# The last seven pivots of a small triangular solve move from GpSimd to VectorE

## The reference

```python
kk = jnp.einsum('bhncd,bhnsd->bhncs', k, k)
A = jnp.where(strict, beta[..., :, None] * kk * decay, 0.0)
rhs = jnp.concatenate([v * beta[..., None], k * (beta * jnp.exp(G))[..., None]], axis=-1)
sol = lax.linalg.triangular_solve(eye + A, rhs, left_side=True, lower=True)
```

## Time and profile before

| | |
|---|---|
| median of 3 runs | 2664.82 us (2664.16 to 2670.57) |
| the profiled execution | 2664.91 us, of which the span of its instructions is 2663.4 us |
| PE, PE weight loads | busy 96%, 95% of the span |
| DVE, ACT, POOL | busy 62%, 50%, 20% |
| TensorE clock granted, mean | 0.987 |
| DMA | 189 GB/s of memory traffic over the span |

### The profile page before, as it was taken

How to read it: one execution, slowest core, us unless ns; L and a number is a source line. 1 busy time by engine, 2 the same in 40 slices (tenths; PEclk the granted TensorE clock), 3 DMA queues, 4 the chain that set the end, 5 groups by cost and what they waited for, 6 DMA issues and landing times.

```text
span 2663.4 us, 53087 instructions
## 1 busy us (share of the span) xinstructions
PE 2566.9 (96%) x20849; PEld 2540.5 (95%) x20849; DVE 1661.4 (62%) x2866; ACT 1337.6 (50%) x2030; POOL 529.2 (20%) x910
## 2 busy tenths in 40 slices
PE   6999999999999999999999999999999999999997
PEld 5899999999999999999999999899999999999997
DVE  4858677676867675533355565466676656776665
ACT  5546455464645544443344343355555545665563
POOL 1335271634527160000000000100110000110100
PEclk9999999999999999999999999999999999999999
DMA  5555464655546456667645556656997567986563
GB/s 178 165 144 170 138 189 134 179 149 163 165 140 193 133 167 185 189 197 216 202 154 171 181 166 203 217 167 217 312 311 236 180 198 228 320 284 194 167 194 112
DMA packets 444289, 506.58 MB, mean 190 GB/s; under 512 B 21145, under 2 KB 423714, under 8 KB 441298
## 3 DMA queue, kind: packets, MB, share of 16 engines
q1 hardware_dynamic: 416128, 415.42, 51.9%
q0 software_dynamic: 27408, 88.53, 10.6%
q10 hardware_dynamic: 578, 0.19, 0.0%
HBM read 478.15 MB, written 26.49 MB: 189 GB/s over the span
## 4 chain that ended last, share of the span: by engine, by line
PE 60%; DMA 2%; POOL 1%; issue 1%; DVE 1%; ACT 0%; DVEq 0%; POOLq 0%; ACTq 0%
PE bank L695 60%; DMA raw<-in_w_o 1%; POOL sol L558 1%; POOL prod L555 1%; DMA raw<-in_w_ffn_down 0%; DVE wlo L1302 0%; PE bank L720 0%; ACT whi L982 0%; DMA raw<-in_w_ple_gate 0%; DMA DT<-sol_scratch 0%; DVEq L234 0%; DMA sol_scratch<-sol 0%; DVE xlo L1330 0%; POOL sol_scratch L588 0%; POOL sol L551 0%
## 5 line engine op out<-in xcount | busy, mean ns | idle before, releaser
L695 PE MATMUL bank<-xhi,whi 128*128 128x264 f32 x5520 | 1597.8, 289 | 37.1 <-DVE wlo L1302 16.9
L695 PE MATMUL bank<-xlo,whi 128*128 128x264 f32 x5520 | 1572.7, 285 | 0.0
L695 PE MATMUL bank<-xhi,wlo 128*128 128x264 f32 x5520 | 1570.3, 284 | 0.0
L1302 DVE TENSOR_TENSOR wlo<-raw,whi 128x1024 fp32r<-128x1024 f32 x828 | 1012.8, 1233 | 752.5 <-ACT whi L982 751.6
L982 ACT ACTIVATE whi<-raw 128x1024 fp32r<-128x1024 f32 x828 | 872.7, 1058 | 811.9 <-PE bank L695 728.1
L695 PEld LDWEIGHTS bank<-xhi,whi 128*128 128x128 f32 x5520 | 1046.5, 190 | 41.3 <-issue 40.6
L695 PEld LDWEIGHTS bank<-xlo,whi 128*128 128x128 f32 x5520 | 1046.9, 190 | 2.2 <-issue 1.9
L695 PEld LDWEIGHTS bank<-xhi,wlo 128*128 128x128 f32 x5520 | 1043.4, 189 | 0.0
L695 PE MATMUL bank<-ahi,whi 128*128 128x264 f32 x704 | 200.7, 285 | 2.5 <-DVE wlo L1302 2.5
L695 PE MATMUL bank<-ahi,wlo 128*128 128x264 f32 x704 | 200.8, 285 | 0.0
L695 PE MATMUL bank<-alo,whi 128*128 128x264 f32 x704 | 200.3, 285 | 0.0
(11 more groups left out here) (294 smaller groups left out, 1862.0 us busy)
## 6 DMA issues: line engine op xcount, KB each, us to landing
raw<-in_w_in SPq DMA_DIRECT2D x356, 512.0 KB, 4.0
raw<-in_w_ffn_gate SPq DMA_DIRECT2D x88, 512.0 KB, 5.0
raw<-in_w_ffn_up SPq DMA_DIRECT2D x88, 512.0 KB, 4.6
raw<-in_w_ffn_down SPq DMA_DIRECT2D x96, 384.0 KB, 3.4
raw<-in_w_gdn_out SPq DMA_DIRECT2D x64, 512.0 KB, 3.6
chunkS<-in_state_gdn POOLq DMA_DIRECT2D x16, 1024.0 KB, 7.2
raw<-in_w_sconv_out SPq DMA_DIRECT2D x32, 512.0 KB, 3.6
raw<-in_w_o SPq DMA_DIRECT2D x32, 512.0 KB, 3.8
```

Source lines behind the costliest of these rows:

```text
L695: return pe.matmul(out, lhsT, rhs, start=start, stop=stop)
L1302: dve.tensor_tensor(wlo[:, at_ % SPLIT, :, :], raw[:, at_ % RAW, :, :], f32(whi[:, at_ % SPLIT, :, :]), ALU.subtract).then_inc(lo_ready, 1)
```

## The change

POOL stops after pivot 23 and signals `begun`. A new DVE step `solve`, written into slot 21 behind the split of piece 24, waits for `begun`, does pivots 24 to 30 with the same two operations a pivot, and signals `solved`, for which POOL waits before it stores `sol`. POOL's copy of the unit columns is written ahead of the wait for `blk`.

```diff
+LASTP = 24
...
-        DVE_STEP = {"cur": {0: ("exponents",), 5: ("lt",), 13: ("qn",), 16: ("qkt",), 26: ("mask",), 27: ("e0",),
+        DVE_STEP = {"cur": {0: ("exponents",), 5: ("lt",), 13: ("qn",), 16: ("qkt",), 21: ("solve",), 26: ("mask",), 27: ("e0",),
...
             def solve(grp):
 
+                mine.inc(pool.tensor_copy(sol[:, :, :], unit[:, :, :]))
                 pool.wait_ge(g["blk_in"], grp * 64 + 64)
                 pool.sem_inc(pool_passed, 1)
-                mine.inc(pool.tensor_copy(sol[:, :, :], unit[:, :, :]))
-                for j in range(SB - 1):
+                for j in range(LASTP):
                     n, m = SB - 1 - j, j // 4 + 1
...
                 mine.settle(pool)
-                pool.sem_inc(g["solved"], 1)
+                pool.sem_inc(g["begun"], 1)
...
+                elif slot == "solve":
+                    dve.wait_ge(g["begun"], gr + 1)
+                    for j in range(LASTP, SB - 1):
+                        n, m = SB - 1 - j, j // 4 + 1
+                        mine.inc(dve.tensor_tensor(prod[:, 0:m, 0:n], blk[:, j, j + 1:SB].unsqueeze(1).to_broadcast([P, m, n]),
+                                                   sol[:, 0:m, j:j + 1].to_broadcast([P, m, n]), ALU.mult))
+                        mine.settle(dve)
+                        mm_ = dve.tensor_tensor(sol[:, 0:m, j + 1:SB], sol[:, 0:m, j + 1:SB], prod[:, 0:m, 0:n], ALU.add)
+                        if j < SB - 2:
+                            mine.inc(mm_)
+                            mine.settle(dve)
+                    mm_.then_inc(g["solved"], 1)
```

More of the change, by code:

```diff
@@ L248, in trunk @@
         act_self, dve_self, pool_self = sem("act_self"), sem("dve_self"), sem("pool_self")
-        pool_passed, dve_passed = sem("pool_passed"), sem("dve_passed")
+        pool_passed = sem("pool_passed")
         ident_ready = sem("ident_ready")
@@ L269, in trunk @@
             "rows", "gb", "expo", "dt", "kcopied", "lt", "nturned", "ncopied",
-            "blk_stored", "blk_in", "solved", "sol_stored", "dt_in", "vturned", "vcopied", "pt", "masked",
+            "blk_stored", "blk_in", "begun", "solved", "sol_stored", "dt_in", "vturned", "vcopied", "pt", "masked",
             "t0", "t0c", "pt0", "e0", "pe0", "f0c", "pf0", "u0", "s1", "s1c", "ks", "r",
```

## The result

| | before | after |
|---|---|---|
| median, us | 2664.00 (20 runs, 2657.1 to 2670.57) | 2671.91 (20 runs, 2663.84 to 2681.62) |
| ratio, 95% interval | | **1.0033** (1.0025 to 1.0041) |
| the profiled execution, us | 2664.91 | 2681.62 |
| PE's waits for `DT`, us | 19.5 in 8, longest 6.2 | 25.1 in 8, longest 4.4 |
| falls of the clock behind `pt` | 3 (groups 0, 2, 6) | 6 (groups 0, 2, 3, 4, 5, 6) |

The change makes the kernel 0.33% slower.

The account below looks back on a forecast made before the run. PE, busy 96% of the span, was taken as the bound, with 19.5 us of waits for `DT` to shrink. Gains of 3.6 (group 0), 4.5 (groups 1 to 7) and 3.2 (clock), 11.3 us, gave 2653.6 us, range 2646.5 to 2661.5.

Parts of the forecast that it names:

- the fourteen operations: DVE's pivots 24 to 30, two chained operations each, take 3.1 us in all, between 2.8 and 4.4.
- dear and cheap small operations: Rivals on DVE's operations: dear, up to 0.31 us each, 2675.2 us, chance 0.05; cheap, 0.09 us each, 2641.3 us, chance 0.03.
- what sets the end of the solve: Group 1: DVE's program place, not POOL, sets it; `begun` comes 4.0 us before split 24 ends; store 0.64 us earlier.
- group 0 up to the store: Group 0: DVE waits for POOL, `begun` comes at about 139.95, and the store starts at 143.8, 4.9 us earlier.
- the change doesn't do what it says: Rival: copy hidden in one group of eight, group 0's pivot 23 no sooner; 2655.1 us, inside the forecast, no separate chance.
- PE does not wait for split 25: Split 25, delayed behind DVE's pivots, still has 4 us to spare in group 1 and 2.6 in group 0; costs nothing.
- the step that took the time from store to `DT` as constant: Store to `DT` stays 11.8 us as in group 1; piece 29's load, up to 3.5 us later, costs nothing.
- 4.5 us: Groups 1 to 7: the store of `sol` starts 0.64 us earlier in each, a gain of 4.5 us in all.
- The prediction's own sign of being wrong: Wrong if PE's `DT` waits exceed 15 us, DVE takes over 3.7 us, or PE waits for `wlo` at piece 25.
- two falls of the clock go: Behind `pt` of groups 2 and 6: waits shrink to about 1.4 us, so two clock falls vanish, gaining 3.2 us.
- group 0, wait and clock: Group 0's wait for `DT` shrinks to 2.6 us, gaining 3.6 us, between 2.8 and 4.9; its clock fall is left in.
- given back by the transfers: Rival: in groups 1 to 7 late loads fall on the store and cancel the 0.64 us; 2661.3 us, chance 0.20.

Follow-up runs that it names:

- wait_only: Kernel before, with DVE in groups 1 to 7 waiting for POOL's whole solve ahead of split 25, doing no pivot: 2663.36 us, ratio 0.9995.
- both_no_dve: Kernel before without pivot 30, and piece 29's load held in groups 1 to 7 until POOL's second store DMA is issued: 2669.75 us, ratio 1.0011.
- hold_loads: Changed kernel, with SP holding the load of piece 29, and all behind it, until the store of `sol` has landed: 2670.77 us, ratio 1.0015.
- late_copy: Changed kernel with the copy of the unit columns put back behind the wait for `blk`: 2671.88 us, ratio 1.0015.
- hold_dt: Piece 29's load held until `DT` landed: in before 2661.66 us, in after 2652.02, in after with POOL going on to pivot 27 2644.74.

## Why the prediction was wrong

**Right: the fourteen operations.** 3.12 us in group 1 (260.63 to 263.75), 3.1 forecast. Two of the four rivals, dear and cheap small operations, are out by this.

**Right: what sets the end of the solve.** In group 1 POOL's pivot 23 ends at 256.31 and split 24 at 260.72: DVE had nothing to wait for. The store comes 0.63 us earlier against the split (0.64 forecast).

**Right: group 0 up to the store.** Pivot 23 ended at 140.05 (139.95 forecast), the store started at 143.90 (143.8). The shorter multiplication of pivot 23 (0.28 us for 1.28) and the hidden copy are both there: the copy ran at 110.12 and the first pivot at 112.61. So the rival that the change doesn't do what it says is out as well.

**Right: PE does not wait for split 25.** The fourteen operations cost PE no wait for `wlo`.

**Wrong: the step that took the time from store to `DT` as constant, and costed the shifted loads at nothing.** The prediction asked whether the late load of piece 29 would be *needed* too early, and found slack. It did not ask what the load would fall *onto*. The term "4.5 us" of groups 1 to 7 was -0.63 on the solve and +1.66 on the trip, in the mean of the seven groups: +7.2 by those means, and 20.73 - 13.24 = +7.5 us by the waits. The prediction's own sign of being wrong, waits for `DT` of more than 15 us in all, came with 25.1. In group 0 the same term, 11.8 us from the store to `DT`, was 13.8, so its wait was 4.36 us and not 2.6.

**Wrong: "two falls of the clock go".** They were to go since the waits would sink below 1.7 us. The waits of those groups rose instead, and groups 3, 4 and 5 lost the clock as well: +4.9 us where -3.2 was forecast, and group 0 lost 0.9 more behind `pt`. In group 4 that is chance: it waited 2.37 us and fell, where before it waited 2.53 and did not.

| term, us | forecast | profiled execution |
|---|---|---|
| group 0, wait and clock | -3.6 | -1.9 + 0.9 = -1.0 |
| groups 1 to 7, waits | -4.5 | +7.5 |
| groups 1 to 7, clock | -3.2 | +4.9 |
| sum | -11.3 | +11.4 |

The medians differ by +7.9 us; the profiled execution shows the direction and the parts, not the typical size.

**The rival "given back by the transfers"** named this mechanism, loads held back by late splits and falling onto the store, and had 0.20. What was wrong in it was its bound: it let the loads take back the 0.64 us and no more. Before's own trace had shown how long the trip took when loads fell on it in one way, and nothing bounded another way. Since the trip grew by 1.7 us, the rival had the wrong sign. The row that could have warned is the load of piece 29 at 263.5, 2.0 us ahead of a store at 265.46: one that is "up to 3.5 us later" crosses it.

**What stays open.** The runs show that the loads of weights lengthen the trip (8.6 to 8.9 us with them held, 11.8 and 13.5 beside them), and that with an earlier store and later loads together it is longer than before without DVE's pivots too (12.6 and 13.2 us). Each of the two alone gave +0.56 and +0.42 us, which one profile each can't tell from scatter. They don't show what share of the lengthening is the sum of the bytes and what the bunching of two loads 1.1 us apart. Whether DVE's own operations add anything to the trip was not shown either; if they do, it is within the scatter of some 0.6 us. How much of after's 0.33% the mechanism makes without DVE's pivots stays open, since wait_only and both_no_dve were not measurably slower than before.

## What to carry to other kernels

A small round trip through memory that runs beside a prefetch stream need not have a fixed duration (here its means went from 8.6 to 14.2 us): ask of every edit how it shifts the loads against the trip, since an in-order engine that is held up by 3 us also holds up the loads which it releases. Hold the loads back from such a trip where the buffers allow, and then look at what stands in program order behind the first consumer of the held load. Where a stage has only a fraction of a us to win, measure it with a real lead (here one slot or three pivots more) before judging the idea.

## What was not expected of the hardware

- The trip of `sol` through memory (four stores and four fetches) takes 8.6 to 8.9 us in the mean with the weight loads held, 11.8 in before and 13.5 in after. The store alone landed in 3.6 to 3.7 us in most groups of hold_loads, in 5.1 to 6.1 beside the loads in before, and in 5.9 to 7.7 in after. So about three microseconds of before's trip already come from the loads beside it.
- The mean trip of two kernels that do the same around the store, after and late_copy, differed by 0.6 us between their two profiled executions: as much as the change wins on the solve.
- The waits for `DT` of before, of after and of nine of the experiments (the three hold_dt kernels aside), 88 in all, show what came before a fall of the clock to the lower level: none of the 42 of up to 1.87 us brought a fall, all 17 of 2.89 us and over did, and of the 29 between them 15 did, the shortest of 1.88 us and the longest harmless one of 2.85. The 2 us that the prediction called safe are not quite, and above it chance reaches as far as 2.9 us.
- In group 3, in every one of these kernels, the fourth DMA of POOL's store is issued some 2 us late, so its trip is longer also where nothing else is in the way (10.0 to 10.2 us in the hold_dt kernels, whose other groups take 8.0 to 9.7). No run here shows why.
